# Expert kernel on one core: the sixteen upper-half products of a unit in another order of chunks

## What is computed

```python
s1 = q[..., :128] @ k1.T ; s2 = q[..., 128:] @ k2.T     # 8 heads, 128 keys each
...                                                     # top 16 of the sums, eid = e1 * 128 + e2
a  = gelu(u_tab[eid] . h)                               # 16384 single-neuron experts
out = sum_k (softmax(top sums) * a)_k * v_tab[eid]_k
```

## Time and profile before

| | |
|---|---|
| median of 3 runs | 2240.01 us (2239.88 to 2240.08) |
| the profiled execution's own time | 2239.02 us |
| its span, first to last instruction | 2237.3 us |
| mean granted TensorE clock | 0.999 |
| TensorE matmul records / weight loads, share of the span | 99% / 93% |
| VectorE / ScalarE / GpSimd, share of the span | 76% / 60% / 38% |
| matmuls, and as many weight loads | 15792 |

### The profile page before, as it was taken

One profiled execution on the slowest core, in us unless ns is written; L12 is line 12 of the kernel. 1 busy time (PEld: TensorE's weight loads), 2 busy tenths in 40 slices (PEclk: granted clock), 3 DMA queues, 4 the chain that ended last, 5 costly groups with the idle time before them and its releaser, 6 DMA issues.

```text
span 2237.3 us, 49289 instructions
## 1 busy us (share of the span) xinstructions
PE 2216.5 (99%) x15792; PEld 2082.9 (93%) x15792; DVE 1704.3 (76%) x3283; ACT 1353.4 (60%) x2705; POOL 854.4 (38%) x766
## 2 busy tenths in 40 slices
PE   8999999999999999999999999999999999999998
PEld 8999999999999888888999999999999998888887
DVE  6556768976888788788874567699578888888887
ACT  6544546667777555555764545566677775555555
POOL 3100108988777122121032001099877771221210
PEclk9999999999999999999999999999999999999999
DMA  6444554555444789888555445455554448898884
GB/s 225 162 143 164 168 181 160 188 186 181 159 159 160 259 306 324 271 304 298 176 187 164 141 166 188 137 189 187 183 178 159 159 161 284 311 321 267 306 279 138
DMA packets 127141, 462.94 MB, mean 207 GB/s; under 512 B 14704, under 2 KB 14864, under 8 KB 126288
## 3 DMA queue, kind: packets, MB, share of 16 engines
q1 hardware_dynamic: 106416, 385.20, 49.1%
q0 software_dynamic: 20640, 76.68, 12.1%
HBM read 457.87 MB, written 3.95 MB: 206 GB/s over the span
## 4 chain that ended last, share of the span: by engine, by line
PE 96%; DVE 2%; ACT 1%; issue 1%; POOLq 0%; POOL 0%; ACTq 0%; DVEq 0%
PE ps L1436 21%; PE ps L1441 20%; PE ps L1437 20%; PE ps L1674 10%; PE ps L1675 10%; PE ps L1676 10%; PE ps L1630 1%; PE ps L1631 1%; PE ps L1589 1%; PE ps L1552 0%; DVE w_lo L875 0%; POOLq L324 0%; DVE h_lo L914 0%; PE ps L1554 0%; PE ps L1535 0%
## 5 line engine op out<-in xcount | busy, mean ns | idle before, releaser
L398 POOL TENSOR_TENSOR w_lo<-raw,w_hi 128x512 fp32r<-128x512 f32 x508 | 644.9, 1292 | 251.9 <-ACT w_hi L499 156.3
L1436 PE MATMUL ps<-h_hi,w_hi 128*128 128x256 f32 (+1 forms) x2592 | 651.2, 289 | 10.1 <-DVE h_lo L856 7.9
L1437 PE MATMUL ps<-h_lo,w_hi 128*128 128x256 f32 (+1 forms) x2592 | 638.3, 282 | 0.0
L1436 PEld LDWEIGHTS ps<-h_hi,w_hi 128*128 128x128 f32 x2592 | 489.3, 189 | 11.5 <-issue 9.3
L1437 PEld LDWEIGHTS ps<-h_lo,w_hi 128*128 128x128 f32 x2592 | 487.8, 188 | 0.2
L477 ACT ACTIVATE w_hi<-raw 128x1024 fp32r<-128x1024 f32 x334 | 351.8, 1053 | 190.5 <-PE ps L1441 189.7
L1244 DVE TENSOR_TENSOR w_lo<-raw,w_hi 128x512 fp32r<-128x512 f32 x504 | 347.6, 690 | 120.4 <-ACT w_hi L725 83.0
L875 DVE TENSOR_TENSOR w_lo<-raw,w_hi 128x1024 fp32r<-128x1024 f32 x208 | 256.5, 1233 | 186.7 <-ACT w_hi L477 185.7
L1674 PE MATMUL ps<-w_hi,h_hi 128*128 128x512 f32 x1016 | 395.2, 389 | 0.0
L1676 PE MATMUL ps<-w_hi,h_lo 128*128 128x512 f32 x1016 | 395.2, 389 | 0.0
L1675 PE MATMUL ps<-w_lo,h_hi 128*128 128x512 f32 x1016 | 395.2, 389 | 0.0
(11 more groups left out here) (225 smaller groups left out, 2973.5 us busy)
## 6 DMA issues: line engine op xcount, KB each, us to landing
raw<-stream SPq DMA_DIRECT2D x730, 512.0 KB, 3.4
bias<-bias_in POOLq DMA_DIRECT2D x2, 1152.0 KB, 6.9
x_keep<-x POOLq DMA_DIRECT2D x2, 1152.0 KB, 5.3
x<-x_keep POOLq DMA_DIRECT2D x2, 1152.0 KB, 10.5
x<-x_in SPq DMA_DIRECT2D x4, 288.0 KB, 4.6
y_out<-t_op SPq DMA_DIRECT2D x4, 288.0 KB, 2.1
ws<-ws_in POOLq DMA_DIRECT2D x2, 512.0 KB, 4.2
ring<-u_rows,rows POOLq DMA_INDIRECT x44, 6.5
```

The lines of the kernel that those rows point to most:

```text
L398: return pool.tensor_tensor(w_lo[:, k % 2, lo_col:hi_col], raw[:, k, lo_col:hi_col], w_hi[:, k % 2, lo_col:hi_col].bitcast(F32), ALU.subtract)
L1436: pe.matmul(out, wh, rhs_hi, start=first, stop=False)
L1437: pe.matmul(out, wh, rhs_lo, start=False, stop=False)
```

## The change

A table WOVEN gives for each of the sixteen upper-half products its chunk and its part (0 is hi, 1 is lo). Both loops of the first expert stage issue the products in the order of the table and no longer chunk by chunk. The chunks' parities in that order are even, even, odd, even, odd, odd, twice, then even, even, odd, odd. In the mixing quads the test for the place of a group is made on products and no longer on chunks. Lower halves, waits and the other stages are as before.

```diff
--- before.py
+++ after.py
@@ -59,6 +59,8 @@
 PLE_BANK = [0, 0, 6, 2]
 GATE_BANK = [0, 1, 2, 3, 5, 6, 7, 3]
 PREPS = 8 * C + CP
+WOVEN = [(0, 0), (0, 1), (1, 0), (2, 0), (1, 1), (3, 0), (2, 1), (4, 0), (3, 1), (4, 1), (5, 0), (5, 1),
+         (6, 0), (6, 1), (7, 0), (7, 1)]
 PAIRED = [0, 2, 1, 3, 4, 6, 5, 7]
 T_OPS = 4 * C
 HALF = KEYS // 8
@@ -1436,6 +1438,12 @@
                     pe.matmul(out, wh, rhs_hi, start=first, stop=False)
                     pe.matmul(out, wh, rhs_lo, start=False, stop=False)
 
+                def woven(out, j, n):
+
+                    c, part = WOVEN[n]
+                    rhs = prompt_lo[L][c] if part else prompt_hi[L][c]
+                    pe.matmul(out, w_hi[:, j % 2, c * P:c * P + P], rhs, start=(n == 0), stop=False)
+
                 def with_lower(out, j, col, rhs_hi, last):
 
                     return pe.matmul(out, w_lo[:, j % 2, col:col + P], rhs_hi, start=False, stop=last)
@@ -1600,8 +1608,8 @@
                             out = ps[:, j, 0:SEQ]
                             pe.wait_ge(evac, e0 + i * 4 + (4 * Q_U + j + 1))
                             pe.wait_ge(hi, u0 + i * 4 + (4 * Q_U + j + 1))
-                            for c in range(C):
-                                with_upper(out, j, c * P, prompt_hi[L][c], prompt_lo[L][c], c == 0)
+                            for n in range(2 * C):
+                                woven(out, j, n)
                             pe.wait_ge(lo_half, L * LOWS + i * 4 + (j + 1))
                             for c in PAIRED[0:C // 2]:
                                 m = with_lower(out, j, c * P, prompt_hi[L][c], False)
@@ -1637,9 +1645,9 @@
                         out = ps[:, j, 0:SEQ]
                         pe.wait_ge(evac, e0 + i * 4 + (4 * (Q_U + U_TOP + U_ONLY) + j + 1))
                         pe.wait_ge(hi, u0 + i * 4 + (4 * (Q_U + U_TOP + U_ONLY) + j + 1))
-                        for c in range(C):
-                            with_upper(out, j, c * P, prompt_hi[L][c], prompt_lo[L][c], c == 0)
-                            if group_behind[j] == c + 1:
+                        for n in range(2 * C):
+                            woven(out, j, n)
+                            if 2 * group_behind[j] == n + 1:
                                 group(i, j)
                         for c in range(C):
                             if c == 0:
```

## The result

The changed kernel takes **2244.84 us** (median of 15 runs, 2244.18 to 2246.09) where the kernel before takes 2239.88 us (15 runs, 2239.39 to 2240.53): a ratio of 1.0022, 95% interval 1.0015 to 1.0029, or +4.96 us. It lies in the stated range (2232.0 to 2249.5), but the forecast of no change with a lean to -1.5 us was wrong: the kernel is slower, by the side of the rival named there as the lost pattern.

The account below looks back on a forecast made before the run. TensorE was taken as the bound. Weights 0 and places -1.5 us took the profiled 2239.02 us to 2237.5; as that execution lies 1.0 us below the median, the forecast was 2238.5 us, range 2232.0 to 2249.5.

Parts of the forecast that it names:

- the lost pattern: Rival: the new order breaks the upper half's cycle of four, steps 0.1187 us, +7.7 us, 2247.7 us; slower by over 0.2%: 0.30.
- What bounds the kernel: Both expert stretches: TensorE busy for all but 0.15 and 0.05 us, clock 1.00; no other engine sets the pace.
- Part 1, weights: Upper-half products: loading a weight tile twice in a row saves nothing, so parting the twins costs 0.
- Part 2, places: Upper half's even and odd chunks: one more short even-to-odd step a unit, -0.0058 us times 256, -1.5 us.
- mirror image: Upper half: short step belongs to the row following an even row, three in place of four, +1.5 us; with forecast 0.30.
- order is indifferent: Rival for upper-half steps: how many products come from each place counts, not their order; 0 us, 2240.0 us; chance 0.16.
- every crossing is cheap: Rival: every upper-half change between even and odd takes the short step, -9.0 us, 2231.0 us; faster by over 0.2%: 0.24.
- decision point: Test for the slower rival: a unit's upper half over 1.887 us, 0.0175 us more, times 256 is 4.5 us, 0.2%.

Follow-up runs that it names:

- e1: Changed kernel with weight tiles in the woven order but moving operands in the order of before: 2240.00 us, ratio 1.000.
- e13: Changed kernel, all sixteen upper-half moving operands at column 0 of chunk 0, weight tile starts turning 0, 0, 32, 32 columns: 2245.18 us.
- e14: Changed kernel, upper-half moving operands from chunk 0 and weight tiles both turning their starts together by 0, 0, 32, 32 columns: 2245.00 us.
- e6: Changed kernel, all sixteen upper-half moving operands at column 0 of chunk 0, weights in the order of before: 2253.62 us.
- e2: Changed kernel with moving operands in the woven order but weight tiles in the order of before, each twice in a row: 2244.78 us, ratio 1.0020.
- e3: Changed kernel with upper-half places in strict alternation, even, odd, even, odd, weights with their chunks: 2245.64 us, ratio 1.0027.
- e4: Changed kernel with eight upper-half products from even chunks, then eight from odd ones, weights with their chunks: 2250.03 us, ratio 1.0045.
- e5: Changed kernel, upper-half moving operands from chunk 0 with start columns 0, 0, 32, 32 four times, weights in the order of before: 2241.07 us.
- e7: Order of the kernel before, with h_hi and h_lo starting 64 bytes later in SBUF by pads: 2264.59 us.
- e8: Order of the kernel before, with h_hi and h_lo starting 128 bytes later in SBUF by pads: 2260.69 us.
- e11: Order of the kernel before, with h_hi and h_lo starting 96 bytes later in SBUF by pads: 2270.09 us.
- e12: Order of the kernel before, with h_hi and h_lo starting 32 bytes later in SBUF by pads: 2270.11 us.

## Why the prediction was wrong

**What bounds the kernel: right.** TensorE without a wait, at the same clock, in all runs; 256 units x 0.020 us is 5.1 us, the measured 4.96.

**Part 1, weights: right.** Price 0; e1 shows 0.1 us, which is within the noise.

**Part 2, places: the failed step.** The prediction took the step from an even to an odd operand for the owner of the short step ("the pair of this and the next is the natural owner of a price") and multiplied by one crossing more: -5.8 ns a unit, where the unit grew by 20 ns, 15 in the upper half and 5 in the lower one. In the changed kernel four of the five even-to-odd crossings take 118 to 119 ns; the short steps are the second (even to odd), the seventh (even to even) and the thirteenth (even to even). Its mirror image, a short step for the row behind an even one, had the sign and the count right (three in place of four), though not their positions, and priced the loss at 5.8 ns a unit. The deeper fault is common to both: they took a step's time for a price of its own, to be counted, when what the rows show is the sum of a cycle. One short step fewer accounts for 6 ns, thirteen longer steps for 9, and the lower half for 5 ns that neither reading had.

**Weights and moving operand as a pair.** The prediction said that a product's cost should belong to it and the load beside it. e13 and e14 support a part of the weights in it; the inference from it, that the crossing is what counts, did not follow.

**The rival "order is indifferent": wrong**, and with it what I made of the earlier trace rows. At 288 columns natural order and cycle differ by less than the reading, and that was carried over to 256 columns. There alternation costs 1893 - 1867 = 26 ns in sixteen steps. The rule of the Trainium skill that spoke for it (TensorE: Matmul & The Clock Gate, section "Step-by-step: what each phase is for"), that fetching the next weights takes nothing from the matmul's stream, does not agree with these runs: with the moving operands untouched, weights that start 128 bytes further on half of the time take sixteen steps from 1901 to 1883 ns (e6, e13). Its consequence in the prediction, that no order of places could matter, is refuted by e2 and e3.

**The rival "the pattern is lost": the one that came.** Its decision point was 0.0175 us a unit, the measured value is 0.020. Its price, taken from units out of step, was 0.030 for the upper half (1.90 against 1.87); measured was 0.015, since the new order keeps three short steps and is not without a pattern, and 0.005 in the lower half, where the bound for full loss was 0.019. With the size of 0.020 the rival's time is 2245, with its own 2247.7. **The rival "every crossing is cheap": wrong**; e3, with eight crossings from even to odd and eight back, is 5.8 us slower than the kernel before and not faster.

**Evidence that was there.** The units of the earlier trace rows have the order of before and not its steps. The prediction read them as needing most of their sixteen products to fall back into the cycle; their starts say more. The unit of 337.40 is in the cycle from its lower half on, the one of 720.11 not within its sixteen. Nor are they typical: behind a group the kernel before has 203, 117, 117, 118, 119, 113, 117, 118 ns (medians), so the cycle is back with the second four. All of them show that a step's time depends on more than its neighbours. That speaks against any price for each crossing, and I used it for the rival alone. It should have moved the forecast to the slower side.

**Still open.** Why the cycle of four is the best of the six orders, and what exactly the moving stream and the weight load contend for, if they do. That they contend is what e6, e13, e14 and the four shifts point to; no run isolates it. A stream of matmuls without weight loads was not tried.

## What to carry to other kernels

In this kernel, with TensorE as the bound and operands four bytes wide, moving h by 32 to 128 bytes against the weights cost 0.9 to 1.4%, and other orders of places 0.2 to 0.6%. Other widths were not tried. A new small tensor ahead of an operand in SBUF can turn this knob by accident, as the pads did: after adding a buffer, compare the steps of an untouched stage before judging the edit. Read a repeating pattern of steps as one sum over its cycle; don't price its single steps and recombine them. An order of places is found by measuring whole orders, in each surrounding in which they run, and one that breaks a cycle can also cost something in the products behind it (5 ns in the lower half of the changed kernel, 12 in e4, nothing in e3).

## What the runs showed of the hardware that was not expected

- A shift of the moving operand's start by 128 bytes is a different place: with one chunk and starts 0, 0, 32, 32 the pattern and the 2800 ns of the kernel before come back (e5); with one start only, steps settle at 120.0 ns from the ninth on (e6), 3% above the cycle's 116.7.
- 32 to 128 bytes of pad ahead of two tensors cost 20.8 to 30.3 us of 2240 (e7, e8, e11, e12), most of it in 512-column products that went from 226.4 to between 232.2 and 234.0 ns, with TensorE shown as fully busy before and after.
- In the kernel before 117 of the 118 units are 2800 ns long and one 2799, in the changed one all 118 are 2820, with VectorE, ScalarE, GpSimd and the transfers at work beside them; nothing of those shows in TensorE's steps. It is not so for every layout: with h shifted by 96 bytes (e11) the units lie between 2829 and 2843 ns.
